# Even attention on one core: scores three units ahead, PSUM banks by kind of job, modulation jobs spread over the loop

## What is computed

```python
def even_mixer(hx, hc, w_in, w_out, rpb, dw, dw_b, ln_g, ln_b, ctx_out):
    px = hx @ w_in
    qx, kx, vx, ux, gx = jnp.split(px, ...)
    pc = hc @ w_in
    qc, kc, vc, uc, gc = jnp.split(pc, ...)
    a_x = neighbourhood_attention(heads(qx), heads(kx), heads(vx), kc, vc, rpb)
    b_x = conformer_conv(ux * jax.nn.sigmoid(gx))
    y_x = jnp.concatenate([a_x, b_x], axis=-1) @ w_out
    a_c = context_attention(heads(qc) * A_HEAD_DIM ** -0.5, kc, vc)
    b_c = conformer_conv(uc * jax.nn.sigmoid(gc))
    y_c = jnp.concatenate([a_c, b_c], axis=-1) @ w_out
```

## Time and profile before

| | |
|---|---|
| profiled execution, us | 1027.61 |
| its span, us | 1025.9 |
| median of three runs, us | 1028.89 |
| TensorE busy | 949.1 us, 93% |
| VectorE busy | 401.2 us, 39% |
| ScalarE busy | 248.7 us, 24% |
| mean granted TensorE clock | 0.982 of full speed |

### The profile page before, as it was taken

One profiled execution on the slowest core, in us unless ns is written; L12 is line 12 of the kernel. 1 busy time (PEld: TensorE's weight loads), 2 busy tenths in 40 slices (PEclk: granted clock), 3 DMA queues, 4 the chain that ended last, 5 costly groups with the idle time before them and its releaser, 6 DMA issues.

```text
span 1025.9 us, 17384 instructions
## 1 busy us (share of the span) xinstructions
PE 949.1 (93%) x5919; PEld 599.9 (58%) x5920; DVE 401.2 (39%) x883; ACT 248.7 (24%) x538; POOL 211.7 (21%) x306
## 2 busy tenths in 40 slices
PE   5999999979998899998988899999988999998886
PEld 3444458545886555555555474877875555555553
DVE  4159494563837111110101379565344212221124
ACT  5120002545324222221222240032133111111112
POOL 1008400110001243332322100000003333332320
PEclk9999999999999899998999999999999999999999
DMA  9984555896426799999999999984557997999996
GB/s 358 317 264 174 180 160 206 290 314 242 170 73 236 252 404 405 406 406 407 408 406 407 353 359 395 291 310 121 193 185 255 400 395 293 406 404 404 404 406 255
DMA packets 129079, 315.80 MB, mean 308 GB/s; under 512 B 28891, under 2 KB 59891, under 8 KB 128996
## 3 DMA queue, kind: packets, MB, share of 16 engines
q1 hardware_dynamic: 113200, 295.87, 77.6%
q0 software_dynamic: 10800, 12.72, 3.6%
q10 hardware_dynamic: 4996, 6.09, 1.7%
HBM read 315.00 MB, written 22.31 MB: 329 GB/s over the span
## 4 chain that ended last, share of the span: by engine, by line
PE 73%; DMA 13%; DVE 5%; SPq 3%; issue 3%; ACT 2%; POOLq 0%; DVEq 0%; POOL 0%; ACTq 0%
PE ps L1169 18%; PE ps L973 16%; DMA ring<-in_moe_w 11%; PE ps L1025 8%; PE ps L1195 8%; PE ps L983 5%; SPq L732 3%; PE ps L1141 3%; PE ps L917 2%; PE ps L1179 1%; DMA ring<-in_w_mod 1%; PE ps L1346 1%; PE ps L1528 1%; PE ps L1546 1%; DVE small L2485 1%
## 5 line engine op out<-in xcount | busy, mean ns | idle before, releaser
L1169 PE MATMUL ps<-ring,RT 128*64 128x256 f32 x2128 | 257.4, 395 | 25.0 <-DMA ring<-in_moe_w 21.0
L1169 PEld LDWEIGHTS ps<-ring,RT 128*64 128x64 f32 x2128 | 161.6, 142 | 96.2 <-issue 25.3
L973 PE MATMUL ps<-RT,ring 128*128 128x512 f32 (+1 forms) x544 | 182.1, 493 | 1.2 <-ACT RT L1703 0.6
L973 PEld LDWEIGHTS ps<-RT,ring 128*128 128x128 f32 x544 | 102.2, 190 | 77.3 <-issue 70.7
L2296 DVE TENSOR_TENSOR RT<-RT,ps 64x256 f32<-64x256 f32 x64 | 27.0, 423 | 273.1 <-ACT RT L1774 273.1
L1195 PE MATMUL ps<-ring,RT 128*64 128x512 f32 x424 | 100.5, 593 | 2.5 <-DVE RT L2302 1.7
L1774 ACT ACTIVATE RT<-ps 64x256 f32<-64x256 f32 x64 | 24.2, 378 | 256.7 <-PE ps L1169 256.7
L2461 DVE SCALAR_TENSOR_TENSOR RAB<-RM,chan,RAB 128x512 f32<-128x512 f32 x120 | 79.7, 744 | 0.0
L2715 POOL DMA_INDIRECT pair_out<-RH,sidx_all x62 | 62.8, 1013 | 55.4 <-POOL sidx_all L2712 52.7
L2703 POOL DMA_INDIRECT RH<-hrow,sidx_all x56 | 59.2, 1058 | 49.4 <-POOL sidx_all L2700 49.4
L2691 POOL DMA_INDIRECT RH<-hrow,idx x7 | 7.8, 1119 | 296.7 <-DVE idx L2248 189.5
(11 more groups left out here) (298 smaller groups left out, 1025.9 us busy)
## 6 DMA issues: line engine op xcount, KB each, us to landing
ring<-in_moe_w SPq DMA_DIRECT2D x358, 512.0 KB, 13.4
ring<-in_w_mod SPq DMA_DIRECT2D x96, 512.0 KB, 9.2
ring<-in_odd_w_in SPq DMA_DIRECT2D x24, 512.0 KB, 9.8
ring<-in_even_w_in SPq DMA_DIRECT2D x20, 512.0 KB, 10.8
ring<-in_even_w_out SPq DMA_DIRECT2D x8, 512.0 KB, 8.5
RAB<-in_moe_w SPq DMA_DIRECT2D x8, 512.0 KB, 6.8
RAB<-pair_out SPq DMA_DIRECT2D x8, 512.0 KB, 7.8
ring<-in_odd_w_out SPq DMA_DIRECT2D x8, 512.0 KB, 7.1
```

What stands on the lines that cost most here:

```text
L973: mm = pe.matmul(bank, w[:, c, P * ft:P * (ft + 1)], moving[:, c, :], start=(c == 0), stop=(c == NCH - 1))
L1169: mm = pe.matmul(bank[CAP * k:CAP * (k + 1), 0:BLK], xt(c), w[k][:, BLK * c:BLK * (c + 1)], start=(c == 0), stop=(c == NCH - 1))
```

## The change

- `S_AHEAD` goes from 2 to 3. Scores, maxima and exponentials of units 0 and 1 still come ahead of the values' projection (`S_EARLY`), those of unit 2 behind it, and those of unit n + 3 in turn n.
- PSUM banks are given by kind of job: scores of unit n take banks 2 * (n % 3) and the next one; transposed probabilities take banks 6 and 7 (units 0 and 1 of a pair), 6 (unit 2) and 7 (unit 3); latent sums and columns take 7, context sums and modulation take 6. The value projection has named banks too. Context units' transpositions fill one bank and not parts of two.
- The four modulation vectors come after turns 2, 6, 10 and 14 and not after 1, 3, 5 and 7; their columns after turns 3 and 7 and not 2 and 4.
- `OC` of a head pair comes at the end of its own turn 3, behind `scores`, and not in the turn after.
- Behind the attention the banks go on from bank 1, as before.

```diff
-S_AHEAD = 2
+S_AHEAD = 3
+S_EARLY = 2
...
-MOD_AFTER = {2 * m + 1: lv for m, lv in enumerate(MOD_ORDER)}
-COL_AFTER = {2: (0, 3), 4: (0, 4)}
+MOD_AFTER = {4 * m + 2: lv for m, lv in enumerate(MOD_ORDER)}
+COL_AFTER = {3: (0, 3), 7: (0, 4)}
+
+
+V_BANK = {(0, 0): 4, (0, 1): 5, (1, 0): 7, (1, 1): 4}
+PT_BANK = (6, 6, 6, 7)
...
+    def scores(n):
+        add(("S", n), "act", 2, bank=2 * (n % 3))
...
+    for n in range(S_EARLY, S_AHEAD):
+        scores(n)
     for n in range(UNITS):
-        add(("PT", n), "act", 2)
+        add(("PT", n), "act", 2 if n % 4 < 2 else 1, bank=PT_BANK[n % 4])
         if n % 4 == 2:
-            add(("OL", n // 4), "act")
-        if n % 4 == 0 and n:
-            add(("OC", n // 4 - 1), "act")
+            add(("OL", n // 4), "act", bank=7)
         if n + S_AHEAD < UNITS:
-            add(("S", n + S_AHEAD), "act", 2)
+            scores(n + S_AHEAD)
         if n in MOD_AFTER:
-            add(("mod",) + MOD_AFTER[n], "dve")
+            add(("mod",) + MOD_AFTER[n], "dve", bank=6)
+        if n % 4 == 3:
+            add(("OC", n // 4), "act", bank=6)
         if n in COL_AFTER:
-            add(("col",) + COL_AFTER[n], "dve")
-    add(("OC", 3), "act")
+            add(("col",) + COL_AFTER[n], "dve", bank=7)
+    jobs.append(("next bank", 1, None))
...
# TensorE
+            for n in range(S_EARLY, S_AHEAD):
+                scores(n)
             mods = iter(range(len(MOD_AFTER)))
             for n in range(UNITS):
                 probs_T(n)
                 if n % 4 == 2:
                     weighted("OL", n // 4)
-                if n % 4 == 0 and n:
-                    weighted("OC", n // 4 - 1)
                 if n + S_AHEAD < UNITS:
                     scores(n + S_AHEAD)
                 if n in MOD_AFTER:
                     modulation(*MOD_AFTER[n], at["mod"] + 4 * next(mods))
+                if n % 4 == 3:
+                    weighted("OC", n // 4)
                 if n in COL_AFTER:
                     columns_of(*COL_AFTER[n])
-            weighted("OC", 3)
...
# ScalarE
+            for n in range(S_EARLY, S_AHEAD):
+                exps(n)
...
                 if qt == 2:
                     head_outputs("OL", hp)
-                if qt == 0 and hp:
-                    head_outputs("OC", hp - 1)
+                if qt == 3:
+                    head_outputs("OC", hp)
                 if n + S_AHEAD < UNITS:
                     exps(n + S_AHEAD)
...
# VectorE
-            for n in range(S_AHEAD):
+            for n in range(S_EARLY):
                 maxima(n)
             normalise(0)
+            for n in range(S_EARLY, S_AHEAD):
+                maxima(n)
```

More of the change, by code:

```diff
@@ L247, in psum_plan @@
     plan, drained, last_of_bank, at = {}, {"act": 0, "dve": 0}, {}, 0
-    for n, (name, who, wide) in enumerate(jobs):
+    n = 0
+    for name, who, wide in jobs:
+        if name == "next bank":
+            at = who
+            continue
         if placed[name] is None:
@@ L253, in psum_plan @@
         else:
-            banks = [placed[name]]
+            banks = [placed[name] + k for k in range(wide)]
         drained[who] += 1
@@ L259, in psum_plan @@
             last_of_bank[b] = name
+        n += 1
     return plan
@@ L580, in bank_of, with turned_bank_of @@
             return ps[:, bank, :] if wide == 1 else ps[:, bank:bank + wide, :]
+        def turned_bank_of(n):
+            bank = bank_of(("PT", n))
+            return bank if n % 4 < 2 else bank.rearrange("p (h k) -> p h k", h=2)
         def full(eng, *name):
@@ L1418, in probs_T @@
             def probs_T(n):
-                bank = open_bank("PT", n)
+                open_bank("PT", n)
+                bank = turned_bank_of(n)
                 pe.wait_ge(probs_ready, n + 1)
+                k0 = 0 if n % 4 < 2 else 2
                 for hh in (0, 1):
-                    for kt in range(0 if n % 4 < 2 else 2, 4):
-                        mm = pe.transpose(bank[:, hh, P * kt:P * (kt + 1)], PROBS[n % 3][:, hh, P * kt:P * (kt + 1)], ident)
+                    for kt in range(k0, 4):
+                        mm = pe.transpose(bank[:, hh, P * (kt - k0):P * (kt - k0 + 1)], PROBS[n % 3][:, hh, P * kt:P * (kt + 1)], ident)
                         freed(mm)
@@ L1921, in _ @@
             act.wait_ge(conv_step, 4 * TAPS)
+            for n in range(S_EARLY, S_AHEAD):
+                exps(n)
             for n in range(UNITS):
                 hp, qt = n // 4, n % 4
-                bank = full(act, "PT", n)
+                full(act, "PT", n)
+                bank = turned_bank_of(n)
                 if qt == 0 and hp:
@@ L1931, in _ @@
                 else:
[L1932 removed]
+                    drain(PTC[:, :, :, P * (qt - 2):P * (qt - 1)], bank.rearrange("p h (k q) -> p h k q", k=2))
                 if qt == 2:
                     head_outputs("OL", hp)
[L1935 to L1936 removed]
+                if qt == 3:
+                    head_outputs("OC", hp)
                 if n + S_AHEAD < UNITS:
```

6 lines of the change are left out of this document (2 added, 4 removed).

## The result

| | before | change |
|---|---|---|
| median, us | 1028.98 (1026.93 to 1030.77, 5 runs) | 1043.01 (1042.21 to 1047.48, 5 runs) |
| profiled execution, its span | 1027.61, 1025.9 | 1044.31, 1042.5 |
| mean granted clock | 0.982 | 0.977 |

The change is slower: ratio 1.0147, 95% interval 1.0135 to 1.0159. Between the medians lie 14.0 us, between the two profiled executions 16.7.

What follows compares the result with a forecast made beforehand. TensorE is busy 93% of the span, and the attention's gain or loss should reach the end one for one. Attention ending at 254.8, not 242.7, adds 12.1 to 1027.6: 1039.7, put at 1040 us; range 1036.8 to 1044.3.

Steps and rivals of the forecast that it cites:

- the slots' return: End of mod(0,5), which frees the slots mod(1,2)'s loads wait for; forecast at 208.9 us, before at 197.0.
- the gap: TensorE idle ahead of mod(1,0), from 220.0 us until ScalarE's drain at 233.8; forecast 13.8 us.
- the clock: Granted clock of 0.50 after the gap: the first 3.6 us of mod(1,0) do 1.8 us of work, 1.8 lost.
- The 18 and 24.8 us bounds for the tables: Both ends for the time from the slots' return to masked tables of heads 6 and 7; 20.7 us was taken.
- the transpositions and waits up to mod(0,5), 4.3 us: Waits on TensorE from 179.4 us to mod(0,5)'s end, mostly for drains: 4.3 us on top of 25.2 of work.
- The walk: The three engines' orders followed with the trace's durations; for before it ended the attention at 242.8, trace 242.65.
- waits of 3.1 in the tail: TensorE's waits from the drain at 233.8 us to the attention's end, beside 16.2 of work; largest 1.6 ahead of unit 14.
- The start at 179.4: Start of the attention from which TensorE's work was summed, with 0.64 us for unit 2's scores awaiting the last value bank.
- its rival of a short table transfer: The 4.57 us between heads 6 and 7 were other traffic; tables 16.1 us after the slots' return, 1035.1 us; chance 0.04.
- Tables in time: Rival: without the tables' wait the attention ends at 239.5, 3.2 us sooner, giving 1024.4 us; chance 0.04.
- Absorbed delay: Rival: the delay is taken up behind the attention by experts that wait for DMAs anyway, about 1028.5 us; chance 0.03.
- Banks dearer than walked: Rival: transpositions sharing one bank pair wait for drains, doubling the walked waits, 7.4 us more, 1047 us; chance 0.05.

Runs made afterwards that it cites:

- e1: The change with the tables of heads 6 and 7 ahead of mod(1,2)'s loads in SyncE's queue; 1035.81 us, ratio to before 1.0013.
- r2: The change again, no edit, on another chip than e1; 1048.34 us, ratio to before 1.0141.
- e9: The change with only the number by which TensorE waits for ScalarE's drain of OC corrected, every engine's order kept; 1048.01 us, ratio to before 1.0141.
- e10: The change with tables of heads 6 and 7 ahead of mod(1,2)'s loads and OC's drain count corrected; 1032.68 us, ratio to before 0.9995.
- r1: The kernel before again, no edit, on another chip than e1; 1033.60 us, ratio to before 1.0001.
- e3: The change's banks and lead alone, modulation vectors and columns at before's turns; 1048.00 us, ratio to before 1.0131.
- e2: The kernel before with only the change's later turns for modulation vectors and columns; 1035.62 us, ratio to before 1.0014.
- e4: The change with 28 extra products keeping TensorE busy in the gap ahead of mod(1,0); 1050.86 us, ratio to before 1.0160.

## Why the prediction was right

**What held.** The mechanism, step by step: SyncE's unmoved order puts the tables of heads 6 and 7 behind loads that wait for mod(0,5)'s slots; unit 12's bias is then late, and VectorE, ScalarE's drain and TensorE stand in a row. e1 takes this away and nothing of the loss is left. The tables were ready 21.05 us after the slots' return (20.7 forecast), the drain came 4.3 us behind them (4.2), the gap was 13.2 us (13.8), the clock cost 1.6 us (1.8), and from the mean to the end nothing was lost or won. The 18 and 24.8 us bounds for the tables held.

**How near the edge it was.** The attention and its entry cost 16.2 us where 12.1 were forecast: the sum was a quarter too small. The range reaches 15.4 us above before. The first medians lie 14.0 us apart; by the ratios it is 15.1 us in the first pair and 14.6 in r2, with intervals that reach past the range, and the spans of the two pairs of profiles differ by 16.6 and 16.2. So the mechanism held, and the number came inside with little to spare. The range itself has a slip of 0.3 us: its lower end is reckoned from 1040, its upper end from 1039.7.

**The missed size.** The attention ended at 258.89 and not at 254.8. The 4.1 us lie in these terms:
- "the transpositions and waits up to mod(0,5), 4.3 us". The slots came back 29.9 us after the first scores and not 28.9. More than half of it is the first of the three waits by count, 0.84 us, of which e9 leaves 0.31. The walk used the drain's own time, where the semaphore counts.
- "waits of 3.1 in the tail": they were 4.06, and the 1.38 us at unit 12's transpositions is the third such wait. e9 has 0.47 there.
- The start at 179.4. The first scores came at 181.40, where 180.04 was expected with the value bank's wait. Between nine profiles of kernels with the change's banks and lead they came at 180.5 to 181.7, in five with before's at 179.2 to 180.4. 1.4 us on average is twice the 0.64 that I walked; what the rest is stays open.
- 0.35 for the tables, 0.1 for the drain behind them, and 0.3 of small ones in the tail.

**Right in sum, wrong in its parts.** The 20.7 us were 12.4 for the weights, 1.4, 4.57 between the heads and 2.36. In the trace head 6's masks began 16.4 us after the slots' return and head 7's came without any wait behind them: the two transfers ran together, and landed late, head 7's 1.4 us behind head 6's. Then all eight masks took 4.6 us. The prediction had no term for head 6's own four masks, 2.4 us, because in before they were hidden in the 4.57; its rival of a short table transfer, which puts the 4.57 at nothing, should have come to 18.5 us and not 16.1. That 20.7 came out near 21.05 is luck. The rival is refuted all the same, at 21.05 us. With the rate of the weights gone from the queue at 223.5 us and the tables still under way, its share was 0.50 at 41 and 64 GB/s (the half microseconds above, 225.5 to 226.5). The Trainium skill, "DMA: Bandwidth & Descriptors", "Why small descriptors are slow (HBM only)", would have 256-byte runs lose a quarter; this trace has them at a sixth to a tenth of the weights' 405 GB/s.

**The other rivals.** Tables in time: e1 shows what it is worth, 63.3 us, level with before; of the 3.2 us of gain that I gave it, waits by count took 2.3 (63.3 in e1, 61.0 in e10). With the count mended e10 is 2.7 us shorter than r1, but its mean still comes 3.1 us behind the walk's 239.5: 1.5 us are the later start, 1.6 are waits that were not walked. Absorbed delay: refuted, 783.6 against 783.3 us. Banks dearer than walked: true by about 2 us, a quarter of what that rival had; e3 shows that waits for drains, with the low clock behind them, would be the main cost had the vectors stayed at their turns.

## What to carry to other kernels

When a job is moved later, follow what its end releases in every queue: here the price was not in the moved work but in small transfers that stood in a fixed order behind the loads waiting for its buffers, and two lines of that order were worth 14 us. Where waits go by a count, the number must be that of the draining engine's order; if the plan's order differs, the wait ends with a job that has nothing to do with the buffer, and the trace shows it as a releaser from the wrong line. And read a small edit in its own stretch: here the stretches behind it moved the total by more than the edit did.

## What the runs showed that I had not expected

- Kernels with the same code behind the attention take 782 to 792 us there. It is not only a matter of one execution: e1 and e2 ran on one chip, their medians are 1035.81 and 1035.62, and their means come at 243.76 and 252.11, so e1's stretch is some 8 us longer in the median as well. But one kernel is not fixed there either: before has 783.3 us in its first profile and 787.5 in r1.
- In the change the sixteen DMAs of the eight tables, 96 KB each, took 5.1 to 11.3 us from issue to landing. The four of heads 6 and 7 kept SyncE for 5.62 us, where eight loads of 512 KB were issued in 3.96 us (e1).
- TensorE's clock stayed at 1.00 through 13 us in which it did no useful work but ran products (e4), and in the change it fell to 0.50 within 3.1 us of TensorE's becoming idle, while DMAs were still running.
